# One scan over a block of eight groups, and rounding of angles on ScalarE, in the state-space layer of a two-part network

## What is computed

```python
dt = exp(log_dt)[:, None]
mag = exp(lam_re * dt)
a_r = mag * cos(lam_im * dt); a_i = mag * sin(lam_im * dt)
# x[t] = a * x[t-1] + bb @ u[t]      (complex, per group and state)
# y[t] = Re(c @ x[t]);  y = gelu(y + d * u);  ab = y @ w_glu;  out = a * sigmoid(b)
```

## Time and profile before

| what | us |
|---|---|
| median of 3 runs | 1941.32 (1940.2 to 1941.61) |
| the profiled execution | 1941.53 |
| its span in the profile | 1939.7 |
| PE busy in the span | 1895.1 (98%) |
| DVE busy | 1225.8 (63%) |
| ACT busy | 931.2 (48%) |
| POOL busy | 321.1 (17%) |

### The profile page before, as it was taken

The page is one execution under the profiler, slowest core; times in us unless marked ns, Lnnn a source line. Parts: engine busy times, 40 slices in busy tenths (PEclk is TensorE's granted clock), DMA queues, the critical chain, the costliest instruction groups (busy, mean ns, idle before and its releaser), DMA issues.

```text
span 1939.7 us, 26606 instructions
## 1 busy us (share of the span) xinstructions
PE 1895.1 (98%) x9236; PEld 1528.2 (79%) x9236; DVE 1225.8 (63%) x1827; ACT 931.2 (48%) x1584; POOL 321.1 (17%) x214
## 2 busy tenths in 40 slices
PE   5999999999999999999999999999999999999998
PEld 3778788888888766788888888788888888777776
DVE  8954443443448788643343449888767867777673
ACT  4864432332335576532232335466545653466673
POOL 6952100000042000200000042022112215000002
PEclk9999999999999999999999999999999999999999
DMA  5213333333332211333332332322222222222222
GB/s 207 49 30 125 92 98 97 97 97 97 96 93 94 76 45 46 96 97 97 97 95 93 96 96 86 93 77 71 77 87 76 70 73 88 86 66 66 66 76 77
DMA packets 54522, 166.97 MB, mean 86 GB/s; under 512 B 13216, under 2 KB 13344, under 8 KB 53920
## 3 DMA queue, kind: packets, MB, share of 16 engines
q1 hardware_dynamic: 54432, 165.78, 28.2%
HBM read 161.30 MB, written 2.10 MB: 84 GB/s over the span
## 4 chain that ended last, share of the span: by engine, by line
PE 82%; DVE 11%; ACT 4%; issue 2%; DMA 1%; SPq 0%; ACTq 0%; DVEq 0%
PE bank L183 14%; PE bank L185 14%; PE bank L184 14%; PE bank L1608 4%; PE bank L1610 4%; PE bank L1609 4%; PE bank L2265 2%; PE bank L2267 2%; PE bank L2266 2%; PE bank L1632 2%; PE bank L1634 2%; PE bank L1633 2%; DVE w_lo L203 1%; PE bank L1686 1%; PE bank L2367 1%
## 5 line engine op out<-in xcount | busy, mean ns | idle before, releaser
L203 DVE TENSOR_TENSOR w_lo<-raw,w_hi 128x1024 fp32r<-128x1024 f32 x286 | 358.7, 1254 | 424.8 <-ACT w_hi L195 422.6
L195 ACT ACTIVATE w_hi<-raw 128x1024 fp32r<-128x1024 f32 x289 | 305.1, 1056 | 381.0 <-DMA raw<-in_w_dram 380.6
L183 PE MATMUL bank<-x1h,w_hi 128*128 128x512 f32 x680 | 266.8, 392 | 0.1
L185 PE MATMUL bank<-x1h,w_lo 128*128 128x512 f32 x680 | 264.8, 389 | 0.0
L184 PE MATMUL bank<-x1l,w_hi 128*128 128x512 f32 x680 | 264.8, 389 | 0.0
L183 PE MATMUL bank<-x0h,w_hi 128*128 128x512 f32 x640 | 250.4, 391 | 0.0
L185 PE MATMUL bank<-x0h,w_lo 128*128 128x512 f32 x640 | 249.0, 389 | 0.0
L184 PE MATMUL bank<-x0l,w_hi 128*128 128x512 f32 x640 | 249.0, 389 | 0.0
L1608 PE MATMUL bank<-x1h,w_hi 128*128 128x512 f32 x384 | 152.7, 398 | 0.6 <-DVE w_lo L203 0.4
L232 POOL TENSOR_TENSOR sq<-h 128x512 f32 x30 | 33.1, 1103 | 723.9 <-DVEq L974 659.7
L183 PEld LDWEIGHTS bank<-x1h,w_hi 128*128 128x128 f32 x680 | 127.9, 188 | 28.0 <-issue 1.2
(11 more groups left out here) (442 smaller groups left out, 3614.5 us busy)
## 6 DMA issues: line engine op xcount, KB each, us to landing
raw<-in_w_dram SPq DMA_DIRECT2D x289, 512.0 KB, 3.6
h<-in_xT_dram SPq DMA_DIRECT2D x1, 2048.0 KB, 12.9
Ur<-in_xu_dram SPq DMA_DIRECT2D x8, 256.0 KB, 2.7
out_dram<-h SPq DMA_DIRECT2D x8, 256.0 KB, 2.3
const<-in_const_dram SPq DMA_DIRECT2D x1, 1028.0 KB, 15.1
B_st<-in_B_dram SPq DMA_DIRECT2D x1, 1024.0 KB, 7.3
C_st<-in_C_dram SPq DMA_DIRECT2D x1, 1024.0 KB, 15.0
p_in<-in_pT_dram SPq DMA_DIRECT2D x1, 1024.0 KB, 4.9
```

The source lines that it names most:

```text
L183: e.matmul(b, w_hi[:, w, k], xh[:, k], start=(k == 0), stop=False)
L185: last = e.matmul(b, w_lo[:, w, k], xh[:, k], start=False, stop=(k == KT - 1))
L195: e.activation(w_hi[:, z], raw[:, z], ACT.Copy).then_inc(hi_split, 1)
L203: e.tensor_tensor(w_lo[:, z], raw[:, z], w_hi[:, z].bitcast(F32), ALU.subtract).then_inc(w_split, 1)
```

## The change

The eight scans of a block become one scan over 8 x 64 = 512 elements. Its decay operand is a row `dec` that ACT copies from `mag8` for each block, with a zero at the first step of each group (set once), so that no state runs over from one group to the next. ACT also computes `k` (angle plus `ROUND`, not yet taken off again) into PSUM bank 7: `k`(0) ahead of `turned(0)`, `k`(1) at the end of turn 0, and `k`(T+1) between `absf` and `sin` of turns T = 1 to 6. DVE keeps one operation, `f` = (k - ROUND) - angle, which is minus the old fraction; the sine's scale changes its sign. As bank 7 is shared, PE's `YT` of block q now waits for `f` of block q+2, and ACT's `k`(t) for `g` of block t-3. At the start, `DI` (L717) goes ahead of `fractions(0)`.

```diff
--- before.py
+++ after.py
@@ -334,7 +334,7 @@
         TB = own_buf("TB", [GB, STEP, SH])
-        TBt = own_buf("TBt", [GB, STEP, SH])
+        dec = own_buf("dec", [2, GB, NSTEP])
         TC = own_buf("TC", [3, GB, STEP + 1, SH])
@@ -355,11 +355,12 @@
         s5_turns = Steps(sem("s5_phase_turns"), "ang", ahead=4)
-        s5_phases = Steps(sem("s5_phases"), "k f", ahead=4)
+        s5_phases = Steps(sem("s5_phases"), "f", ahead=4)
+        s5_whole = Steps(sem("s5_whole"), "k", ahead=4)
         s5_states = Steps(sem("s5_states"), "pr1 pr2 V Z po1 po2 W", ahead=4)
         s5_direct = Steps(sem("s5_direct"), "K Kd", ahead=4)
-        s5_kept = Steps(sem("s5_kept"), "Sx", ahead=4)
+        s5_kept = Steps(sem("s5_kept"), "dec Sx", ahead=4)
         s5_st_kept = Steps(sem("s5_turned_kept"), "ST1 ST2", ahead=4)
@@ -496,7 +497,7 @@
             s = small
-            for counters in (s5_kept, s5_st_kept, s5_k_kept, s5_angles, s5_y_kept, s5_gelu):
+            for counters in (s5_whole, s5_kept, s5_st_kept, s5_k_kept, s5_angles, s5_y_kept, s5_gelu):
                 counters.open(e)
@@ -519,13 +520,24 @@
+            def rounded(t):
+                if t == 0:
+                    e.wait_ge(tables_ready, 2)
+                e.wait_ge(s5_turns.sem, s5_turns.at("ang", t))
+                e.wait_ge(s5_phases.sem, s5_phases.at("f", t - 1))
+                e.wait_ge(s5_gelu.sem, s5_gelu.at("g", t - 3))
+                s5_whole.took("k", e.activation(grid(bank[7]), fractional[t % 2], ACT.Copy, bias=ROUND))
             def turned(t):
                 e.wait_ge(s5_states.sem, s5_states.at("po2", t - 2))
-                s5_angles.took("sin", e.activation(sinb[:, z], fractional[z], ACT.Sin, scale=SIN_SCALE))
+                if 0 < t < NBLK - 1:
+                    rounded(t + 1)
+                s5_angles.took("sin", e.activation(sinb[:, z], fractional[z], ACT.Sin, scale=-SIN_SCALE))
                 e.wait_ge(s5_angles.sem, s5_angles.at("absf", t))
@@ -541,6 +553,14 @@
+            def decay_row(t):
+                if t == 0:
+                    e.wait_ge(decays_kept, 1)
+                    e.wait_ge(zeroed, 3)
+                e.wait_ge(s5_states.sem, s5_states.at("Z", t - 2))
+                s5_kept.took("dec", e.activation(dec[:, t % 2, :, 1:], cut(mag8, t).unsqueeze(2).to_broadcast([LANES, GB, NSTEP - 1]), ACT.Copy))
             def s_kept(t):
@@ -549,9 +569,12 @@
                     st_kept(T)
+                    rounded(0)
                     turned(T)
                     k_kept(T)
+                    decay_row(T)
                     s_kept(T)
+                    rounded(1)
                 elif T < NBLK:
@@ -610,6 +634,7 @@
             e.memset(Wb[:, :, 0:1], 0.0).then_inc(zeroed, 1)
+            e.memset(dec[:, :, :, 0:1], 0.0).then_inc(zeroed, 1)
             for counters in (s5_tables, s5_phases, s5_states, s5_direct, s5_inputs):
@@ -670,14 +695,12 @@
-            whole_turns = grid(bank[6])
             def fractions(q):
                 ff = fractional[q % 2]
-                s5_phases.took("k", ts(whole_turns, ff, ROUND, ROUND, ALU.add, ALU.subtract))
-                s5_phases.next(e, q).took("f", tt(ff, ff, whole_turns, ALU.subtract))
+                e.wait_ge(s5_whole.sem, s5_whole.at("k", q))
+                s5_phases.took("f", stt(ff, grid(bank[7]), ROUND, ff, ALU.subtract, ALU.subtract))
@@ -712,9 +735,9 @@
             e.wait_ge(const_loaded, 16)
-            fractions(0)
             dfull = [SH, SG, SH]
             link(e, tt(DI[:, :, :], d_gain.unsqueeze(2).to_broadcast(dfull), C("id16", rows=SH).unsqueeze(1).to_broadcast(dfull), ALU.mult))
+            fractions(0)
             e.wait_ge(sd_ready, 1)
@@ -749,11 +772,8 @@
                     e.wait_ge(s5_out.sem, s5_out.at("JZ", q - 1))
-                    if q == 0:
-                        e.wait_ge(decays_kept, 1)
-                    for g in range(GB):
-                        last = e.tensor_tensor_scan(Zb[:, g], cut(mag8, q)[:, g:g + 1].to_broadcast([LANES, NSTEP]), turned[:, g], 0.0, ALU.mult, ALU.add)
-                    s5_states.took("Z", last)
+                    flat = lambda b: b.rearrange("p g c -> p (g c)")
+                    s5_states.took("Z", e.tensor_tensor_scan(flat(Zb[:, :, :]), flat(dec[:, z]), bk[3], 0.0, ALU.mult, ALU.add))
                     n().took("po1", tt(grid(bank[6]), Zb[:, :, :], cosb[:, z], ALU.mult))
@@ -787,7 +807,7 @@
             e.sem_inc(norm_mm, 1)
-            e.wait_ge(zeroed, 2)
+            e.wait_ge(zeroed, 3)
@@ -841,6 +861,7 @@
                     e.wait_ge(s5_gelu.sem, s5_gelu.at("g", q - 1))
+                    e.wait_ge(s5_phases.sem, s5_phases.at("f", min(q + 2, NBLK - 1)))
                     for t in range(STEP):
```

## The result

The changed kernel takes 1943.29 us (median of 20 runs, 1941.69 to 1953.00) against 1941.32 for the kernel before in the same 20 rounds (1940.05 to 1942.53): ratio 1.0017, 95% interval 1.0010 to 1.0023. That is 1.97 us slower and within 0.2% of no change; 1943.4 was predicted. The profiled execution took 1942.29 us, 0.76 more than the 1941.53 of the one before.

The account below looks back on a forecast made before the run. Four engines were taken as nearly full, with ACT leading from turn 4; +2.5 on ACT less 0.4 from the last scan gave +2.1 us, 1943.6 for the profiled execution, median 1943.4, range 1939.5 to 1946.0.

Parts of the forecast that it names:

- What a turn loses on DVE: Each turn on DVE: removing `k` saves 0.73 us; one scan of 1.1 us instead of 1.53 gains 0.43.
- What a turn gains on ACT: Each turn on ACT: `k` and `dec` add 0.54 us each, 1.08 together, of which 0.22 is covered in turns 5 and 6.
- The start: Pipeline start: DVE waits for `k`(0), `sq` at 30.4 instead of 29.72, 0.7 us late; start and turn 0 come out even.
- Turn 1: Turn 1: `po1`(0) still ends with POOL's operation, so the scan's 0.43 us is lost; `pr1`(1) comes 0.7 early.
- Turns 2 and 3: Turns 2 and 3: `k`(4) waits for POOL's `ang`(4); `cos`(3) starts at 73.2, `pr1`(3) at most 0.8 us early.
- Turns 4 to 7: Turns 4 to 7: ACT leads; `cos`(4), (5), (6) at 86.2, 98.8, 111.4, `ST1`(7) at 113.1, `Sx`(7) at 119.4, 2.5 us later.
- The signs: Changed profile: ACT without idle time from `ST1`(4) to `Sx`(7), `pr1` of blocks 4 to 6 waiting for `cos`, `cos`(6) near 111.
- The new waits: DVE's `f` waiting for ACT's `k`, and PE's `YT`(q) for `f`(q+2), were costed at nothing.
- rival 4: PE's clock falls once more after longer waits: 17% of 10 us, 1.7 us, giving 1945.1; chance 0.06.
- ACT covering its work: ACT's idle time covers its new work and DVE's gain comes through: 1936.5 at best, about 1939 if half; chance 0.12.
- Nothing moves: Whole stage: the shares cancel because DVE's earlier parts give ACT and PE earlier work, 1941.3; chance 0.15.
- Slow copy: ACT's `dec` takes about 1.1 us, making each of turns 4 to 7 0.5 longer, +2.0: 1945.4; chance 0.12.

Follow-up runs that it names:

- e3: Changed kernel with a second copy of the decay row each turn, into a scratch buffer: 1944.49 us.
- e4: Changed kernel with all eight decay rows copied ahead, in ACT's idle time before turn 2; `k` stays on ACT: 1940.71 us.
- e6: Changed kernel with the weight splits of turns 3, 4 and 5 moved to turns 0 and 1, where ACT waits: 1940.25 us.
- e8: Kernel before the change, with its weight splits of turns 3, 4 and 5 moved to turns 0 and 1: 1941.49 us.
- e2: Changed kernel with the eight scans and without the decay row, so only the rounding `k` moves to ACT: 1942.66 us.
- e10: Changed kernel with one idle product of 512 columns in PE's wait for `ST1`, turns 3 to 7: 1942.64 us.
- e15: Changed kernel with idle products in PE's waits for `ST1` in turns 3 to 7 and ahead of `JS`(7) and `JZ`(7): 1942.76 us.
- e11: Changed kernel with `k`(0) on ACT between `ST1`(0) and `ST2`(0) instead of behind `ST2`(0): 1945.24 us.
- e13: Changed kernel with rows copied ahead, splits in turns 0 and 1, `k`(0) ahead of `ST2`(0), idle products at the stage's end: 1938.69 us.
- e12: Kernel before the change, with idle products ahead of `JZ`(7) and `JS`(7), in PE's waits at the end of the stage: 1940.44 us.

## Why the prediction was right

- **What bounds.** Right. ACT, the least busy of the four in the earlier trace rows, sets turns 4 to 7 of the changed kernel. e3, e4 and e6 against e8 show it by one operation more, one less, and a relief that counts only here. Part of each median's difference is PE's clock, though, and e2 shows that `k`'s wait for the angles has a share.
- **What a turn loses on DVE.** `k` and `f` as taken. The scan was mis-sized: 1.22 us, not 1.1, a gain of 0.31 and not 0.43. By the Trainium skill (DVE: opcode table, instruction layouts, handler registers and perf-mode slots, section 6, Datapath and trigger behaviour) this scan runs at half throughput; the trace agrees, with 1220 ns for 512 elements beside 680 to 690 for an ordinary operation on as many. The 0.1 that was named for this case is what it cost.
- **What a turn gains on ACT.** `dec` 0.61 to 0.63 and `k` 0.60 are the 0.62 and 0.60 taken; the handover is 0.51 to 0.54. Turns 4 to 6 grew by 0.98, 0.75 and 0.76 where 1.08, 0.86 and 0.86 were predicted: 0.1 too much in each.
- **The start.** 30.4 was predicted for `sq`; e10 shows 30.46 and e15 30.54, the changed kernel's own profile 29.22. The step took one value of `ST1`(0) from one profile and didn't ask whether it is the same in each run. The working missed this, and it moves a run by some 1.2 us.
- **Turn 1.** In the early profile `po1`(0) took 0.90 us; in the late ones it took 1.94 (e10) and 1.85 (e15), as the earlier trace rows with 1.80. Right for the case that the rows showed.
- **Turns 2 and 3.** Right in the number and only half right in the cause. `k`(4) waits for `ang`(4) in the changed kernel's own profile (0.21 us idle, `ang`(4) done at 69.24) and in those of e2, e4, e11 and e13. 73.2 for `cos`(3) is 73.18 in e10, but there and in e15 `k`(4) doesn't wait: `ang`(4) is done at 70.47, and `k`(4) starts at 70.72 straight behind `Sx`(3) at 69.73 and `absf`. ACT's own order leads by 0.25 us, and that the angles would have given nearly the same time is luck.
- **Turns 4 to 7.** 86.2, 98.8, 111.4, 113.1 and 119.4 were predicted; e10 has 86.11, 98.58, 111.06, 112.89 and 119.37. In the early profile they are 84.69, 97.15, 109.64, 111.47 and 117.69. From `ST1`(7) to `Sx`(7) are 6.22 there, 6.28 predicted; PE's side wasn't later, as said. The last scan gives back 0.31 and not 0.43.
- **The signs.** One scan of 1.22 us, `f`(0) released by `k`(0), ACT dense but for its short waits for PE between the copies, and `cos`(6) near 111 (109.64, and 111.06 in e10) came as said. `pr1` released by `cos` after a wait, said of blocks 4 to 6, is seen in block 4 alone (0.40); in blocks 5 and 6 the wait has moved to `po2`. A `pr1` without a wait was named as a sign of being wrong. It isn't one here, since the turns are 12.46 and 12.49 us all the same.
- **The new waits.** `f` waiting for `k` cost nothing except at the start, and `YT`'s wait nothing in any profile.
- **Sum.** +2.1 predicted, +1.97 measured. The agreement is better than its parts deserve. The median stands between runs in which PE is at full speed early (1942.29 in the profile, +0.8), runs in which it is late (like e10's 1943.69), and runs up to 1953. For the last ones rival 4 is the natural reading: e3 and e11 show the clock falling behind 2 us waits for `ST1`, and turns that are 2.4 and 3.1 us longer for it (15.77 against 13.4, 15.58 against 12.46), and with idle products in those waits (e10, e15) no run is above 1944.82. The mean granted clock of the runs bears it out for three of the five: 1948.09 and 1948.46 have 0.994, as the profiled executions of e3 and e11 with their falls have, and 1953.00 has 0.991, while every other run of the changed kernel has 0.997 or 0.998. The two runs at 1945.1 are at 0.997 and stay open, and as no profile of the changed kernel caught such a run, where the clock fell in it isn't shown. The rival was put at 0.06 and 1.7 us; by the clock it happened in three of 20 runs, and these lie 5 (two of them) and 10 us above the median.
- **The other rivals.** ACT covering its work: refuted by 12.92 us turns. Nothing moves: e2's and the changed kernel's lower runs come near it, the median doesn't. Slow copy: refuted by the 0.61 of `dec`.

## What to carry to other kernels

Idle share says little about how much an engine can take over: count what a turn of its stream leaves between the wait that opens it and the wait that closes it, and see whether the moved operation can stand there or must stand ahead of what others wait for (alone, the row was free in that place, `k` was not). When work is moved in a software pipeline, look for one-off work that can leave for the idle start; here it paid 3 us, more than the change itself. And a longer wait of TensorE is to be priced twice, once as the wait and once as the slow clock behind it.

## What the runs showed of the hardware

- One scan over 512 elements takes 1220 ns in each of eight, one over 64 elements 260 ns: 2.14 ns for each further element ((1220 - 260) / 448). So joining eight scans saves their overhead, 0.31 us a block, and not more.
- The clock of PE fell behind waits of 2.00 and 2.06 us for `ST1`, and stayed at 1.2 GHz for some 10 us although PE was busy in all of it (the windows of e3 and e11). The three profiles with the order of before (before, e8, e12), where no wait for `ST1` is above 0.99 us, have full clock from 40 to 120 us; so has that of the changed kernel, whose longest wait is 2.00, so such a wait doesn't always bring the fall.
- PE reaches full speed at different times from run to run: pairs of products go from 2.05 to 1.02 us near 19.6 us in the changed kernel's profile and near 21.8 in that of e15, and `ST1`(0) lay between 25.69 and 27.35 us in 14 profiles. The factor of two looks like the two levels of the clock, but the granted clock of the profile reads 1.00 in these windows, so that is an inference. In the kernel before it is hidden behind DVE. Behind the change `sq` follows it, and the 1.2 us between the medians of two groups of runs (e15, 1941.69 and 1942.93) have its size.
- `po1`, with two SBUF inputs one of which comes from the scan, took anything from 0.70 to 2.69 us according to when it meets a POOL operation. Where it was long, it ended 0.55 to 0.56 us after the POOL operation in which it began (blocks 0, 1, 2 and 5 of the changed kernel; e6 with its 2.69), so savings on DVE ahead of it are spent in it.
- In all 14 profiles the execution ended 1803.3 to 1804.0 us after the first weight split behind the stage (L203): what moves in the stage arrives at the end, within 0.7 us.
